# A two-layer decoder step: one more z unit ahead of the first convolution group, a shorter step-size series, two copies moved to ScalarE, and a new order where attention ends

## The chip, the core and the metric

The kernel runs on one core of a Trainium2 chip. The metric is the time of one execution on the device in microseconds (us). A matmul engine (TensorE, PE in the profile), VectorE (DVE), ScalarE (ACT), GpSimd (POOL) and the queue of SyncE (SP) run their own instruction streams, in order, and wait for each other on semaphores.

## The reference, cut to what matters

A Mamba-2 layer and an attention layer, each between two half-size SwiGLU blocks, work on 256 prompt tokens and 8 decode tokens side by side (N = 264 columns everywhere). The change touches the mixers of both.

```python
z, xbc, dt_raw = split(u @ w_in)                       # stage "sin": 49 units of weights
conv = conv_b + sum(xbc_full[:, k:k + t_len] * conv_w[k] for k in range(4))
xbc_act = silu(conv)
dt = softplus(dt_raw + dt_bias)                        # the step sizes, 32 heads
cum = cumsum(dt * a)                                   # per chunk of 128 tokens
decay = exp(where(causal, cum_t - cum_s, -inf))        # then the chunk products
...
s = einsum(q, k) * 64 ** -0.5                          # stage "q", with the shared K/V
prob = softmax(concat([s, sink]))[..., :-1]
out = einsum(prob, v) @ w_o                            # stage "o"
```

## The kernel before, in words

All weights are cut into 128x1024 units that stream through a ring of four buffers: SP loads `raw`, ScalarE rounds it to `whi` (L1080), VectorE subtracts to get `wlo` (L1552), and TensorE multiplies each unit in three passes (L503 to L505), 24 matmuls for a unit. The function `ahead(stage, i, j)` on ScalarE and on VectorE prepares the unit that lies four places on; ScalarE's waits until TensorE has finished unit j.

Stage "sin" is written out by hand in slots `s_`, one unit a slot; `SIN` lists what the slots hold: the step sizes (`dt`), then z units, then groups of four convolution units (c0 to c3, c4 to c7, ...) with z units between. In a slot TensorE runs `sin_unit`, VectorE reads the finished bank (`take`, L1599) and, for the convolution unit before it, runs three taps (`conv_taps`, L1827); ScalarE runs the last tap ahead of them (`tap_last`, L1254) and the silu behind them (`conv_silu`, L1260). From the seventh unit on two banks alternate, so unit j may start only when unit j-2 has been read:

```python
                if j < 7:
                    pe.wait_ge(b_free, sin_bank(j) + 1)
                else:
                    pe.wait_ge(a_free, A0["sin"] + (j - 2 if j < 9 else j + 3))
```

The step sizes go their own way beside that: VectorE computes the softplus by a series of dependent steps on 128x66 (`dt_start`, `dt_series`, `dt_end`, L1796 to L1811), ScalarE gathers them (`gather_sizes`, `gather_steps`), TensorE turns them (`pre_tokens`, slot `PRE_AT`), VectorE copies them out of the bank (L1841, L1842), TensorE forms the sums over tokens (`pre_sums`, from L952), ScalarE copies those (`cum4`, L1368), VectorE makes `tok` and the differences (`pre_sums`, L1853 to L1858; `pre_diff`, L1866), and the first chunk's exponentials follow on ScalarE (`decay_exp(0)`).

In attention eight pairs of heads run as a pipeline: `scores(t)` on TensorE (L667), `maxima(t)` on VectorE (L2090 on), `exps(t)` on ScalarE (L1469), which then puts the mask back into the banks (L1475), `probabilities(t)` on VectorE (L2102 to L2105), `transposes(t)` (L681), `copy_turned(t)` (L1480), `weighted_sum(t)`. The next pairs' rotary turn is `head_mean`, `rope_sin` (L1741) and `rope_add` (L1747) on VectorE. Behind the last queries come `embed_piece(n)` (six matmuls of another projection each) and the decode tokens' attention: `decode_scores` needs the queries that GpSimd spreads (`spread_queries`, L2399, which waits for the last `rope_add`); `decode_maxima` (from L2057), `decode_exp` and `decode_prob` follow. The order is that of the code on each engine.

Of the kernel before, what the change touches and what calls it, by code (L numbers as in the profile page):

```python
# [84 lines left out]
DT_STEPS = 15  # L85
# [5 lines left out]
Z_FIRST = [0, 1, 2]  # L91
Z_AFTER = {0: [3, 4], 1: [5], 2: [6], 3: [7], 4: [8], 5: [9], 6: [10], 7: [11, 12, 13, 14, 15]}
# [6 lines left out]
PRE_AT = 7  # L99
# [65 lines left out]
def trunk_kernel(nc, weights, xT, g1, pT, cst, vec, convst, ssm0, kcT, vc_in, ck, cv,  # L165
# [3 lines left out]
    with ExitStack() as ctx:  # L169
# [102 lines left out]
        pre_d = sem("pre_d")  # L272
        pre_a = sem("pre_a")
# [217 lines left out]
        def _(pe):  # L491
# [455 lines left out]
            def pre_sums():  # L947

                pe.wait_ge(pre_d, 1)
                for c in range(2):  # L950
                    dta = da4[c][:, 0:HEADS]
                    pe.matmul(bank[5][:, 64 * c:64 * c + 32], tri, dta, start=True, stop=True)  # L952
                    pe.matmul(bank[5][:, 64 * c + 32:64 * c + 64], ones, dta, start=True, stop=True)
                    mm = pe.matmul(bank[2][:, 128 * c:128 * c + 128], da4[c], tri, start=True, stop=True)
                mm.then_inc(pre_p, 1)
                pe.wait_ge(pre_d, 2)
                pe.matmul(bank[7][:, 0:256], ones[32:64, :], dgl[32:64], start=True, stop=True)
                pe.matmul(bank[6][:, 0:256], ones[0:32, :], dgl[0:32], start=True, stop=True).then_inc(pre_p, 1)
# [11 lines left out]
            for s_ in range(len(SIN)):  # L970
                if s_ == 1:
                    unit_pair("sin", 0)
                elif s_ > 1:
                    sin_unit(s_)
                if s_ == PRE_AT:
                    pre_tokens()
                if s_ == PRE_AT + 3:
                    pre_sums()
                for g in range(G):
                    if s_ == CHUNK_AT[g] + 3:  # L980
                        add_inter(g)
# [12 lines left out]
                if s_ - 1 in DEC_AT:  # L994
                    decode_columns(DEC_AT.index(s_ - 1))
# [52 lines left out]
            transposes(5)  # L1048
            decode_scores()
            weighted_sum(5)  # L1050
            embed_piece(2)
# [21 lines left out]
        def _(act):  # L1073
# [204 lines left out]
            def select(k):  # L1278

                g, c = k // 2, k % 2  # L1280
                if k == 1:
                    act.wait_ge(pre_d, 5)
# [45 lines left out]
            for s_ in range(SLOTS):  # L1328
# [11 lines left out]
                if 1 < s_ < len(SIN) and s_ != 5:  # L1340
                    ahead("sin", 0, s_)
                if s_ == 4:
                    ahead("sin", 0, 5)
                    gather_sizes()
                if kind == "conv":
# [3 lines left out]
                if s_ == 4:  # L1349
# [16 lines left out]
                if s_ == PRE_AT + 3:  # L1366
                    act.wait_ge(pre_p, 2)
                    act.activation(cum4, bank[2][:, 0:256], ACT.Copy).then_inc(pre_a, 1)  # L1368
                if s_ == PRE_AT + 5:
                    act.wait_ge(pre_d, 4)  # L1370
                    act.wait_ge(pre_const, 1)
                    select(0)
                    act.activation(tok[:, :, :, :], tok[:, :, :, :], ACT.Exp).then_inc(pre_a, 1)
# [172 lines left out]
        def _(dve):  # L1546
# [246 lines left out]
            def dt_series(ks):  # L1793

                for k in ks:
                    dt_step(dve.scalar_tensor_tensor(out=a_, in0=a_, scalar=1.0 / k, in1=s2_, op0=ALU.add, op1=ALU.mult))  # L1796

            def dt_start():
# [6 lines left out]
                dt_step(dve.tensor_scalar(a_, s2_, 1.0 / 17, None, ALU.mult))  # L1805
# [31 lines left out]
            def pre_tokens():  # L1837

                dve.wait_ge(pre_p, 1)
                for c in range(2):  # L1840
                    dve.tensor_copy(dtT[c], bank[4][:, 64 * c + 32:64 * c + 64])  # L1841
                    ins = dve.tensor_copy(da4[c].rearrange("p (k h) -> p k h", k=4), bank[4][:, 64 * c:64 * c + 32].unsqueeze(1).to_broadcast([P, 4, HEADS]))  # L1842
                ins.then_inc(pre_d, 1)
# [109 lines left out]
            for s_ in range(SLOTS):  # L1953
# [26 lines left out]
                if s_ == PRE_AT + 3:  # L1980
                    pre_sums()
                if s_ == PRE_AT + 4:
                    pre_diff(0)
                    pre_diff(1)
                if s_ == PRE_AT + 6:
# [567 lines left out]
```

## Time and profile before

| what | value |
|---|---|
| median of 3 executions | 1197.99 us (1197.15, 1197.99, 1199.66) |
| the profiled execution | 1199.46 us |
| its span, first to last instruction | 1197.6 us |
| PE busy | 1184.5 us (99%) |
| DVE, ACT, POOL busy | 866.2, 699.1, 245.1 us |
| 200 to 300 us (first part of "sin") | PE 98.45, DVE 93.22, ACT 75.93 us busy |
| 900 to 960 us (attention) | PE 57.06, DVE 47.56, ACT 46.63 us busy, mean granted clock 0.97 |

Busy time of PE holds short gaps between pipelined matmuls too, so what counts is when one unit starts after another: 2.90 us when nothing holds it. The profiled execution lies 1.47 us above the median.

### The profile page before, as it was taken

Reading aid. Unit: us, or ns where it says so; the run is one execution under the profiler, and the core shown is the slowest. Engines: PE = TensorE matmul, PEld = TensorE weight load, DVE = VectorE, ACT = ScalarE, POOL = GpSimd, SP = SyncE. Lnnn points to the kernel's source line nnn. Section 1 sums busy time; section 2 is a strip of 40 time slices with the busy share of each in tenths; the row PEclk is TensorE's granted clock in tenths of the full one; section 3 lists DMA queues with packets and bytes.
Section 4 is the critical chain, followed back from the end, with each engine's and each line's share of the span. In section 5 each row is a group of like instructions: output and inputs, shape, how many; then the busy total and the mean of one; then the engine's idle time right before and its main releaser. Section 6 shows DMA issues by size and latency. Waiting matters only on the chain.

```text
span 1197.6 us, 26532 instructions
## 1 busy us (share of the span) xinstructions
PE 1184.5 (99%) x9785; PEld 1156.7 (97%) x9785; DVE 866.2 (72%) x1382; ACT 699.1 (58%) x1148; POOL 245.1 (20%) x352
## 2 busy tenths in 40 slices
PE   9999999999999999999999999999999999999998
PEld 8999999998989899999999999999999899999998
DVE  7667646999899768766745987887468767667448
ACT  6454435787686657555546765555369664444345
POOL 1000002412222202122344333232036310000001
PEclk9999999999999999999999999999999999999999
DMA  8765554755445375867786677657742256555552
GB/s 298 240 209 184 176 178 140 259 184 186 159 149 189 108 225 185 329 211 251 283 294 225 215 276 282 211 184 240 251 141 94 90 171 212 176 179 189 176 178 87
DMA packets 63298, 239.90 MB, mean 200 GB/s; under 512 B 7673, under 2 KB 9633, under 8 KB 58849
## 3 DMA queue, kind: packets, MB, share of 16 engines
q1 hardware_dynamic: 56880, 197.83, 49.5%
q0 software_dynamic: 6064, 40.66, 9.4%
q8 instruction: 41, 0.67, 0.2%
q10 hardware_dynamic: 288, 0.54, 0.1%
q14 instruction: 25, 0.20, 0.0%
HBM read 226.87 MB, written 13.39 MB: 201 GB/s over the span
## 4 chain that ended last, share of the span: by engine, by line
PE 79%; DVE 8%; issue 5%; ACT 5%; DMA 1%; POOL 1%; SPq 0%; DVEq 0%; POOLq 0%; ACTq 0%
PE bank L503 24%; PE bank L504 24%; PE bank L505 24%; ACT whi L1080 2%; DVE wlo L1552 2%; DVE gu L1611 1%; DVE gu L1599 1%; DMA raw<-weights 1%; PE bank L873 1%; PE bank L868 1%; DVE xl L1571 1%; PE bank L895 1%; POOL sq L2179 0%; PE bank L681 0%; DVE xl L1700 0%
## 5 line engine op out<-in xcount | busy, mean ns | idle before, releaser
L1552 DVE TENSOR_TENSOR wlo<-raw,whi 128x1024 fp32r<-128x1024 f32 x367 | 456.3, 1247 | 241.5 <-ACT whi L1080 240.0
L503 PE MATMUL bank<-xh,whi 128*128 128x264 f32 x2008 | 576.1, 287 | 3.3 <-DVE under L1599 1.5
L504 PE MATMUL bank<-xl,whi 128*128 128x264 f32 x2008 | 569.2, 283 | 0.0
L505 PE MATMUL bank<-xh,wlo 128*128 128x264 f32 x2008 | 568.8, 283 | 0.0
L1080 ACT ACTIVATE whi<-raw 128x1024 fp32r<-128x1024 f32 x367 | 385.4, 1054 | 244.3 <-PE bank L505 235.5
L503 PEld LDWEIGHTS bank<-xh,whi 128*128 128x128 f32 x2008 | 378.2, 188 | 7.1 <-DVE wlo L1552 2.7
L504 PEld LDWEIGHTS bank<-xl,whi 128*128 128x128 f32 x2008 | 378.4, 188 | 0.9
L505 PEld LDWEIGHTS bank<-xh,wlo 128*128 128x128 f32 x2008 | 376.6, 188 | 0.0
L503 PE MATMUL bank<-hh,whi 128*128 (+1 forms) x896 | 255.5, 285 | 0.3 <-ACT gu L1435 0.3
L505 PE MATMUL bank<-hh,wlo 128*128 (+1 forms) x896 | 255.0, 285 | 0.0
L504 PE MATMUL bank<-hl,whi 128*128 (+1 forms) x896 | 254.4, 284 | 0.0
L503 PEld LDWEIGHTS bank<-hh,whi 128*128 128x128 f32 x896 | 168.6, 188 | 1.4 <-issue 0.8
L504 PEld LDWEIGHTS bank<-hl,whi 128*128 128x128 f32 x896 | 169.1, 189 | 0.1
L505 PEld LDWEIGHTS bank<-hh,wlo 128*128 128x128 f32 x896 | 168.6, 188 | 0.0
L1146 ACT ACTIVATE hh<-gu 128x264 fp32r<-128x264 f32 (+1 forms) x88 | 37.4, 425 | 168.5 <-DVE gu L1611 168.5
L2179 POOL TENSOR_TENSOR sq<-sq 128x264 f32<-128x264 f32 x49 | 39.7, 811 | 452.0 <-ACT sq L1118 446.7
L1599 DVE TENSOR_TENSOR gu<-bank,rstd 128x264 f32<-128x264 f32 x192 | 82.1, 429 | 16.0 <-PE bank L505 13.1
L1616 DVE TENSOR_TENSOR hl<-gu,hh 128x264 f32 (+1 forms) x88 | 39.6, 450 | 28.7 <-ACT hh L1146 28.7
L2328 POOL TENSOR_TENSOR xact<-xact,da_bc 128x512 f32<-128x512 f32 x32 | 37.8, 1183 | 101.6 <-PE bank L505 99.9
L1827 DVE SCALAR_TENSOR_TENSOR xact<-under,vs,xact 128x256 f32<-128x256 f32 x96 | 47.3, 493 | 2.3
L1611 DVE TENSOR_TENSOR gu<-gu 128x264 f32<-128x264 f32 x88 | 44.2, 502 | 0.0
L2333 POOL TENSOR_TENSOR xact<-xact 128x512 f32<-128x512 f32 x20 | 29.0, 1452 | 60.2 <-PE bank L505 56.4
(333 smaller groups left out, 1017.6 us busy)
## 6 DMA issues: line engine op xcount, KB each, us to landing
raw<-weights SPq DMA_DIRECT2D x367, 512.0 KB, 3.5
under<-ssm POOLq DMA_DIRECT2D x8, 1024.0 KB, 6.9
xact<-ssm POOLq DMA_DIRECT2D x8, 1024.0 KB, 7.2
out_ssm_s<-xact POOLq DMA_DIRECT2D x8, 1024.0 KB, 6.0
xact<-dtx_rows POOLq DMA_DIRECT2D x5, 1024.0 KB, 10.4
zs<-dtx_rows POOLq DMA_DIRECT2D x2, 1024.0 KB, 13.5
x<-xT SPq DMA_DIRECT2D x4, 264.0 KB, 5.5
xact<-stat_rows POOLq DMA_DIRECT2D x2, 528.0 KB, 6.5
```

What stands on the lines that cost most here:

```text
L503: pe.matmul(out, whi[:, w, c], rh, start=start, stop=False)
L504: pe.matmul(out, whi[:, w, c], rl, start=False, stop=False)
L505: return pe.matmul(out, wlo[:, w, c], rh, start=False, stop=stop)
L1080: act.activation(whi[:, s, :], raw[:, s, :], ACT.Copy).then_inc(hi_ready, 1)
L1146: act.activation(dst, gu[:, 2 * p + 1, :], ACT.Copy).then_inc(hh_ready, 1)
L1552: dve.tensor_tensor(wlo[:, s, :], raw[:, s, :], whi[:, s, :].bitcast(F32), ALU.subtract).then_inc(lo_ready, 1)
L1599: dve.tensor_tensor(dst, src[:, 0:N], rstd[:, :], ALU.mult).then_inc(a_free, 1)
L1611: dve.tensor_tensor(gu[:, 2 * p + 1, :], gu[:, 2 * p, :], gu[:, 2 * p + 1, :], ALU.mult).then_inc(h_ready, 1)
L1616: dve.tensor_tensor(one(hl), gu[:, 2 * p + 1, :], one(hh).bitcast(F32), ALU.subtract).then_inc(hl_ready, 1)
L1827: dve.scalar_tensor_tensor(out=out, in0=xr[:, k:k + T], scalar=vs[:, V_CW + CT * k + c:V_CW + CT * k + c + 1], in1=out, op0=ALU.mult, op1= ...
L2179: pool.tensor_tensor(sq3[:, 0, :], sq3[:, 0, :], sq3[:, m, :], ALU.add).then_inc(sq_pair, 1)
L2328: pool.tensor_tensor(by_head(part), by_head(part), da_bc[:, 2 * k:2 * k + 2, 4 * q:4 * q + 4].unsqueeze(3).to_broadcast([P, 2, 4, 64]), AL ...
```

## The change

In "sin" the first convolution group starts one slot later, behind four z units in place of three, and one z unit fewer stands behind it; from slot 9 on the slots hold the same units. The series has three steps on fitted coefficients in place of seven. `PRE_AT` goes from 7 to 8: VectorE's diagonal products, its sums and differences keep or change their slots as below and now stand ahead of the taps of their slot; the copies of the turned step sizes go from VectorE to ScalarE. In attention the order of some calls changes.

```diff
-DT_STEPS = 15
-Z_FIRST = [0, 1, 2]
-Z_AFTER = {0: [3, 4], 1: [5], ...
+DT_STEPS = 11
+ATANH = (0.14006083166778943, 0.14000885871391391, 0.20010764547514603, 0.33333208128558084)
+Z_FIRST = [0, 1, 2, 3]
+Z_AFTER = {0: [4], 1: [5], ...
-PRE_AT = 7
+PRE_AT = 8
@@ TensorE
-                pe.wait_ge(pre_d, 1)
+                pe.wait_ge(pre_t, 1)
...
-                if s_ == PRE_AT + 3:
+                if s_ == PRE_AT + 2:
                     pre_sums()
...
+            embed_piece(2)
             decode_scores()
             weighted_sum(5)
-            embed_piece(2)
@@ ScalarE, slots
-                if 1 < s_ < len(SIN) and s_ != 5:
+                if 1 < s_ < len(SIN) and s_ != 6:
                     ahead("sin", 0, s_)
-                if s_ == 4:
-                    ahead("sin", 0, 5)
+                if s_ == 5:
+                    ahead("sin", 0, 6)
                     gather_sizes()
+                if s_ == PRE_AT + 3:
+                    act.wait_ge(pre_p, 2)
+                    act.activation(cum4, bank[2][:, 0:256], ACT.Copy).then_inc(pre_a, 1)
+                if s_ == PRE_AT + 1:
+                    act.wait_ge(pre_p, 1)
+                    for c in range(2):
+                        act.activation(dtT[c], bank[4][:, 64 * c + 32:64 * c + 64], ACT.Copy)
+                        ins = act.activation(da4[c].rearrange("p (k h) -> p k h", k=4), bank[4][:, 64 * c:64 * c + 32]...)
+                    ins.then_inc(pre_t, 1)
+                if s_ == PRE_AT + 5:
+                    act.wait_ge(pre_d, 3)
+                    act.wait_ge(pre_const, 1)
+                    select(0)
+                    act.activation(tok[:, :, :, :], tok[:, :, :, :], ACT.Exp).then_inc(pre_a, 1)
                 if kind == "conv":
                     tap_last(s_, i)
@@ ScalarE, attention
             exps(6)
-            decode_exp()
             high_o(5)
             embed_copy(2)
+            decode_exp()
             copy_turned(6)
@@ VectorE, slots
+                if s_ == PRE_AT:
+                    pre_tokens()
+                if s_ == PRE_AT + 3:
+                    pre_sums()
+                if s_ == PRE_AT + 4:
+                    pre_diff(0)
+                    pre_diff(1)
                 if last == "conv":
                     conv_taps(li)
...
-                    dt_series((15, 13, 11, 9))
+                    dt_series(ATANH[1:])
                 if s_ == 3:
-                    dt_series((7, 5, 3))
                     dt_end()
-                if s_ == PRE_AT + 1:
-                    pre_tokens()
-                if s_ == PRE_AT + 3:
-                    pre_sums()
...
@@ VectorE, attention
             ahead("q", 0, 5)
+            probabilities(5)
             head_mean(7)
             rope_sin(7)
             rope_add(7)
-            probabilities(5)
-            low_o(4)
             maxima(6)
             decode_products()
+            low_o(4)
+            probabilities(6)
             decode_maxima()
-            probabilities(6)
             low_o(5)
```

ScalarE in stage "sin", from the silu of c2 on. Before, the silu of c2, `whi` for slot 8, then the silu of c3 and the next `whi`:

```order
L1260 ACTIVATE xact<-xact 128x256 [waits conv_sum]
L1080 ACTIVATE whi<-raw 128x1024 [waits unit_used,raw_landed2]
L1260 ACTIVATE xact<-xact 128x256 [waits conv_sum]
L1080 ACTIVATE whi<-raw 128x1024 [waits unit_used,raw_landed3]
L1265 ACTIVATE zs<-zs 128x264 [waits a_free]
L1270 ACTIVATE dact<-gu 128x32 [waits dec_sum]
L1275 ACTIVATE under<-gu 128x2x4 [waits dec_pad]
```

In the changed kernel, where the slots are one later, the same stretch (`small<-bank` are the moved copies):

```order
L1262 ACTIVATE xact<-xact 128x256 [waits conv_sum]
L1082 ACTIVATE whi<-raw 128x1024 [waits unit_used,raw_landed3]
L1353 ACTIVATE small<-bank 128x32 [waits pre_p]
L1354 ACTIVATE small<-bank 128x128
L1353 ACTIVATE small<-bank 128x32
L1354 ACTIVATE small<-bank 128x128
L1262 ACTIVATE xact<-xact 128x256 [waits conv_sum]
L1082 ACTIVATE whi<-raw 128x1024 [waits unit_used,raw_landed0]
```

The four copies now stand behind the silu of c2 and the `whi` of slot 9.

VectorE in stage "sin", from the read of c4 to about the read of c6 (`under<-bank` is the read of a convolution unit, `tok` and `hl<-bank` are the sums, `hl<-hl` the differences). Before:

```order
L1599 TENSOR_TENSOR under<-bank,rstd 128x264 [waits unit_used,tail_copied]
L1552 TENSOR_TENSOR wlo<-raw,whi 128x1024 [waits hi_ready]
L1853 COPY tok<-bank 128x2x32 [waits pre_p]
L1854 COPY tok<-bank 128x2x32
L1855 TENSOR_TENSOR tok<-tok 128x2x32 [waits dve_step]
L1858 TENSOR_TENSOR hl<-bank,hl 32x256 [waits pre_a]
L1858 TENSOR_TENSOR hl<-bank,hl 32x256
L1599 TENSOR_TENSOR under<-bank,rstd 128x264 [waits unit_used,tail_copied,dve_step]
L1827 SCALAR_TENSOR_TENSOR xact<-under,vs,xact 128x256 [waits conv_first]
L1827 SCALAR_TENSOR_TENSOR xact<-under,vs,xact 128x256 [waits conv_sum] x2
L1552 TENSOR_TENSOR wlo<-raw,whi 128x1024 [waits hi_ready]
```

In the changed kernel:

```order
L1608 TENSOR_TENSOR under<-bank,rstd 128x264 [waits unit_used,tail_copied]
L1858 COPY tok<-bank 128x2x32 [waits pre_p]
L1859 COPY tok<-bank 128x2x32
L1860 TENSOR_TENSOR tok<-tok 128x2x32 [waits dve_step]
L1863 TENSOR_TENSOR hl<-bank,hl 32x256 [waits pre_a]
L1863 TENSOR_TENSOR hl<-bank,hl 32x256
L1836 SCALAR_TENSOR_TENSOR xact<-under,vs,xact 128x256 [waits conv_first,dve_step]
L1836 SCALAR_TENSOR_TENSOR xact<-under,vs,xact 128x256 [waits conv_sum] x2
L1561 TENSOR_TENSOR wlo<-raw,whi 128x1024 [waits hi_ready]
L1608 TENSOR_TENSOR under<-bank,rstd 128x264 [waits unit_used,tail_copied]
```

The sums stood ahead of the read of c5, and now stand behind it, ahead of the taps.

VectorE at attention's end, from the `wlo` of `ahead("q", 0, 5)` on. Before (L1730 and L1731 are `head_mean(7)`, L2102 on is `probabilities(5)`, L2090 on is `maxima(6)`):

```order
L1552 TENSOR_TENSOR wlo<-raw,whi 128x1024 [waits hi_ready]
L1730 TENSOR_SCALAR small<-bank 128x1 [waits r_ready,rot_done]
L1731 TENSOR_TENSOR small<-bank,zs 128x4
L1741 TENSOR_TENSOR gu<-under 128x264 [waits q_swapped1]
L1747 TENSOR_TENSOR xact<-gu 128x264 [waits q_sin,q_cos]
L2102 TENSOR_TENSOR small<-small 128x4 [waits s_exp]
L2103 RECIPROCAL small<-small 128x4 [waits dve_step]
L2104 TENSOR_TENSOR under<-under,small 128x2x128 [waits dve_step]
L2105 TENSOR_TENSOR under<-under,small 128x2x256
L2110 TENSOR_TENSOR hl<-bank,hh 128x256 [waits hh_ready]
L2090 TENSOR_REDUCE small<-bank 128x2 [waits s_done]
```

In the changed kernel (L2106 on is `probabilities(5)`, L1739 and L1740 `head_mean(7)`, L2094 `maxima(6)`):

```order
L1561 TENSOR_TENSOR wlo<-raw,whi 128x1024 [waits hi_ready]
L2106 TENSOR_TENSOR small<-small 128x4 [waits s_exp]
L2107 RECIPROCAL small<-small 128x4 [waits dve_step]
L2108 TENSOR_TENSOR under<-under,small 128x2x128 [waits dve_step]
L2109 TENSOR_TENSOR under<-under,small 128x2x256
L1739 TENSOR_SCALAR small<-bank 128x1 [waits r_ready,rot_done]
L1740 TENSOR_TENSOR small<-bank,zs 128x4
L1750 TENSOR_TENSOR gu<-under 128x264 [waits q_swapped1]
L1756 TENSOR_TENSOR xact<-gu 128x264 [waits q_sin,q_cos]
L2094 TENSOR_REDUCE small<-bank 128x2 [waits s_done]
```

The four instructions of `probabilities(5)` went ahead of the rotary turn of the last pair, and `low_o(4)` left the place ahead of `maxima(6)`.

## Rows read from the trace of the kernel before

**Rows 1.** The page, part 1: busy us (share of the span) and instructions.

```profile
PE 1184.5 (99%) x9785; PEld 1156.7 (97%) x9785; DVE 866.2 (72%) x1382; ACT 699.1 (58%) x1148; POOL 245.1 (20%) x352
```

**Rows 2.** Waits of PE: us in total, times, longest.

```profile
PE bank L503 <- DVE under L1599: 1.5, 1, 1.5
PE bank L681 <- DVE under L2105: 1.4, 1, 1.4
PE bank L667 <- ACT bank L1475: 1.3, 3, 0.7
```

**Rows 3.** Timeline of PE in "sin": start, us, instruction, [idle before].

```profile
230.61 0.36 PE L503 MATMUL bank<-xh,whi 128*128 128x264 f32 x1 [1.50 <-DVE under L1599]
...
241.83 0.28 PE L503 MATMUL bank<-xh,whi 128*128 128x264 f32 x1
...
251.56 0.28 PE L503 MATMUL bank<-xh,whi 128*128 128x264 f32 x1
```

**Rows 4.** Timeline of DVE in "sin".

```profile
218.51 1.10 DVE L1796 SCALAR_TENSOR_TENSOR xact<-xact 128x66 f32<-128x66 f32 x4
...
227.12 0.43 DVE L1599 TENSOR_TENSOR under<-bank,rstd 128x264 f32<-128x264 f32 x1
227.47 1.52 DVE L1827 SCALAR_TENSOR_TENSOR xact<-under,vs,xact 128x256 f32<-128x256 f32 x3
228.90 1.22 DVE L1552 TENSOR_TENSOR wlo<-raw,whi 128x1024 fp32r<-128x1024 f32 x1
230.03 0.43 DVE L1599 TENSOR_TENSOR under<-bank,rstd 128x264 f32<-128x264 f32 x1
...
236.51 0.83 DVE L1845 TENSOR_TENSOR xact<-cs,small 32x256 f32<-32x256 f32 x2
...
240.33 0.22 DVE L1853 COPY tok<-bank 128x64 f32<-128x64 f32 x1
...
240.97 0.86 DVE L1858 TENSOR_TENSOR hl<-bank,hl 32x256 fp32r<-32x256 f32 x2
242.13 0.43 DVE L1599 TENSOR_TENSOR under<-bank,rstd 128x264 f32<-128x264 f32 x1 [0.30 <-PE bank L505]
...
249.87 0.42 DVE L1599 TENSOR_TENSOR under<-bank,rstd 128x264 f32<-128x264 f32 x1
```

**Rows 5.** Timeline of ACT in "sin".

```profile
234.90 0.42 ACT L1260 ACTIVATE xact<-xact 128x256 f32<-128x256 f32 x1 [1.60 <-DVE xact L1827]
235.22 1.05 ACT L1080 ACTIVATE whi<-raw 128x1024 fp32r<-128x1024 f32 x1
...
240.14 0.36 ACT L1368 ACTIVATE hl<-bank 128x256 fp32r<-128x256 f32 x1
```

**Rows 6.** Timeline of PE in attention.

```profile
933.64 0.70 PE L667 MATMUL bank<-xact 64*128 64x256 f32 x4 [0.72 <-ACT bank L1475]
...
935.96 1.17 PE L681 MATMUL bank<-cs,under 128*128 128x128 f32 x6 [1.39 <-DVE under L2105]
```

**Rows 7.** Timeline of PE behind `decode_turn`.

```profile
947.17 0.36 PE L503 MATMUL bank<-ph,whi 128*128 128x264 f32 x1
```

**Rows 8.** Timeline of DVE and ACT in attention.

```profile
934.47 0.16 DVE L2102 TENSOR_TENSOR small<-small 128x4 f32<-128x4 f32 x1
...
936.15 0.41 DVE L2090 TENSOR_REDUCE small<-bank 128x2 f32<-128x256 f32 x1
...
937.86 0.45 ACT L1469 ACTIVATE under<-bank,small 128x128 f32<-128x128 f32 x1
...
940.06 0.81 ACT L1475 ACTIVATE bank<-cs 128x768 f32<-128x768 f32 x1
```

**Rows 9.** Timeline of POOL, `spread_queries`, first call (x2).

```profile
923.46 0.78 POOL L2399 TENSOR_SCALAR under<-xact,cs 128x32 f32<-128x32 f32 x2
```

**Rows 10.** The same, second call.

```profile
934.65 1.43 POOL L2399 TENSOR_SCALAR under<-xact,cs 128x32 f32<-128x32 f32 x2 [1.37 <-DVE xact L1747]
```

**Rows 11.** Windows: stretch, us, busy of PE, PEld, DVE, ACT, POOL, granted clock, DMA.

```profile
936.40:939.80 3.40, 3.40 (x30) 3.07 (x30) 1.63 (x7) 2.64 (x9) 3.07 (x8) 0.50 0.03 12
```

More of the change, by code:

```diff
@@ L82 @@
 NV = V_QS + 1
-DT_STEPS = 15
-Z_FIRST = [0, 1, 2]
-Z_AFTER = {0: [3, 4], 1: [5], 2: [6], 3: [7], 4: [8], 5: [9], 6: [10], 7: [11, 12, 13, 14, 15]}
+DT_STEPS = 11
+ATANH = (0.14006083166778943, 0.14000885871391391, 0.20010764547514603, 0.33333208128558084)
+Z_FIRST = [0, 1, 2, 3]
+Z_AFTER = {0: [4], 1: [5], 2: [6], 3: [7], 4: [8], 5: [9], 6: [10], 7: [11, 12, 13, 14, 15]}
 SIN = [("dt", 0)] + [("z", _t) for _t in Z_FIRST]
@@ L272, in trunk_kernel @@
         pre_d = sem("pre_d")
+        pre_t = sem("pre_t")
         pre_a = sem("pre_a")
@@ L955, in pre_sums @@
                 mm.then_inc(pre_p, 1)
-                pe.wait_ge(pre_d, 2)
+                pe.wait_ge(pre_d, 1)
                 pe.matmul(bank[7][:, 0:256], ones[32:64, :], dgl[32:64], start=True, stop=True)
@@ L1281, in select @@
                 if k == 1:
-                    act.wait_ge(pre_d, 5)
+                    act.wait_ge(pre_d, 4)
                 if k >= 2:
@@ L1339, in _ @@
                         decay_exp(2 * CHUNK_AT.index(s_))
-                if 1 < s_ < len(SIN) and s_ != 5:
+                if 1 < s_ < len(SIN) and s_ != 6:
                     ahead("sin", 0, s_)
-                if s_ == 4:
-                    ahead("sin", 0, 5)
+                if s_ == 5:
+                    ahead("sin", 0, 6)
                     gather_sizes()
+                if s_ == PRE_AT + 3:
[5 more added lines that the diff above has]
+                        act.activation(dtT[c], bank[4][:, 64 * c + 32:64 * c + 64], ACT.Copy)
+                        ins = act.activation(da4[c].rearrange("p (k h) -> p k h", k=4), bank[4][:, 64 * c:64 * c + 32].unsqueeze(1).to_broadcast([P, 4, HEADS]), ACT.Copy)
+                    ins.then_inc(pre_t, 1)
[4 more added lines that the diff above has]
+                    act.activation(tok[:, :, :, :], tok[:, :, :, :], ACT.Exp).then_inc(pre_a, 1)
                 if kind == "conv":
@@ L1348, in _ @@
                     decay_exp(2 * CHUNK_AT.index(s_))
-                if s_ == 4:
+                if s_ == 5:
                     gather_steps()
@@ L1365, in _ @@
                     copy_rows(DEC_AT.index(s_))
-                if s_ == PRE_AT + 3:
-                    act.wait_ge(pre_p, 2)
-                    act.activation(cum4, bank[2][:, 0:256], ACT.Copy).then_inc(pre_a, 1)
                 if s_ == PRE_AT + 5:
[L1370 to L1373, printed above, removed]
                     act.wait_ge(pre_p, 3)
@@ L1795, in dt_series @@
                 for k in ks:
-                    dt_step(dve.scalar_tensor_tensor(out=a_, in0=a_, scalar=1.0 / k, in1=s2_, op0=ALU.add, op1=ALU.mult))
+                    dt_step(dve.scalar_tensor_tensor(out=a_, in0=a_, scalar=k, in1=s2_, op0=ALU.add, op1=ALU.mult))
             def dt_start():
@@ L1804, in dt_start @@
                 dt_step(dve.tensor_tensor(s2_, q_, q_, ALU.mult))
-                dt_step(dve.tensor_scalar(a_, s2_, 1.0 / 17, None, ALU.mult))
+                dt_step(dve.tensor_scalar(a_, s2_, ATANH[0], None, ALU.mult))
             def dt_end():
@@ L1837, in pre_tokens @@
             def pre_tokens():
[L1839 to L1843, printed above, removed]
+                dve.wait_ge(dt_a_step, 5)
                 for k in (0, 32):
@@ L1973, in _ @@
                 if s_ == 2:
-                    dt_series((15, 13, 11, 9))
+                    dt_series(ATANH[1:])
                 if s_ == 3:
-                    dt_series((7, 5, 3))
                     dt_end()
-                if s_ == PRE_AT + 1:
-                    pre_tokens()
-                if s_ == PRE_AT + 3:
-                    pre_sums()
[L1982 to L1985, printed above, removed]
+                if s_ == PRE_AT + 5:
                     pre_decode()
```

## The prediction, as it was made before the changed kernel ran

> **What bounds the kernel now.** I read part 1 of the page first. PE is busy for 1184.5 us of a span of 1197.6 [rows 1], so whatever is done elsewhere, the time can only fall by what PE now loses; no matmul is added or taken away. The view of waits then says where PE loses: apart from the start, one wait of 1.5 us for a read by VectorE (L1599), one of 1.4 us for L2105 and three that add up to 1.3 us for L1475 [rows 2]. The timeline places the first in "sin" at 228.8 to 230.6 us [rows 3], the others in attention around 933 to 936 us [rows 6]. A third view, the windows, shows a loss that no wait names: from 936.4 to 939.8 us, just behind two idle stretches of 0.72 and 1.39 us, the granted clock is 0.50 [rows 11], so the score matmuls of the decode tokens run at 1.2 GHz and not at 2.4.
>
> **Stage "sin", why PE waits there.** From c0 on, a VectorE slot is a read, three taps and one `wlo`: 227.12 to 230.03, which is 2.91 us [rows 4]. A unit on PE takes 2.90 us. VectorE therefore never catches up in these slots, and the series of the step sizes had put it behind. Unit 9 needs the read of unit 7, which is c3's at 230.03 to 230.46; PE had been ready at 228.95, and starts at 230.61 [rows 3, 4]. It loses 1.66 us.
>
> **What the first part of the change gives.** Four dependent steps fall away. Four took 1.10 us [rows 4], so everything behind comes 1.1 us sooner. And c3 is now unit 8, not unit 7, so that unit 9 needs only c2's read. In order: the read of z3 at about 221.7 (c0's was at 222.7), then read and `wlo` without taps, 0.35 + 1.13 = 1.48 us, gives c0's read at 223.15 and c1's at 224.6; c1's slot with taps and 0.6 us of waiting for the first tap, which on ScalarE stands behind `whi` and the gather, gives c2's read at 228.2, done at 228.6. PE wants unit 9 at 228.95. **Minus 1.66 us**, and with 0.3 us to spare.
>
> **The copies on ScalarE.** They stand behind the silu of c2 and the `whi` of slot 9, as the order shows. On VectorE c3's read is at 231.1, the diagonal products now come ahead of the taps (0.83 us [rows 4]) and the taps of c2 end at 231.5 + 0.86 + 1.52 = 233.85. ScalarE's silu starts behind them and `whi` 0.32 us later (234.90 to 235.22 [rows 5]); `whi` holds it 0.97 more. The four copies begin at 235.15. Their price is not in the trace: the read of a bank of 256 columns takes 0.36 us (at 240.14, [rows 5]); these have 32 and 128 columns. From below, 4 x 0.1 = 0.4 us, since instructions overlap; from above 4 x 0.36 = 1.4. I take 0.65. So TensorE gets `pre_t` at about 235.8. It gets through units 9 and 10 at 228.95 + 5.8 + 0.1 = 234.9. **Plus 1.0 us** (0.8 to 1.8). What is queued behind that wait is unit 11 and all that follows on PE.
>
> **The sums behind c5's read.** Before, VectorE did them at 240.33 to 241.83 and then still waited 0.30 us for PE to finish c5; they were hidden [rows 4]. Now they stand behind that read, and so do `cum4`'s copy and, on ScalarE, a `whi` that waits for the same unit ahead of it. From c5's read to c7's it took 242.13 to 249.87, 7.74 us. Added: 1.42 us of sums, and 0.37 us in which the last two of them wait for `cum4` (`whi` starts 0.26 us after unit 12, lasts 0.97, the copy 0.36, which ends 1.6 us after unit 12; VectorE is there at 0.30 + 0.35 + 0.64 = 1.3). So c7's read ends 0.30 + 7.74 + 1.79 + 0.42 = 10.25 us after unit 12 starts, and PE starts unit 15, which needs it, 0.14 us on, at 10.39. Now unit 15 starts 251.56 - 241.83 = 9.73 us after unit 12 [rows 3]. **Plus 0.65 us** (0.3 if ScalarE were not late with `cum4`).
>
> The later steps of that chain have room: the first chunk's exponentials follow c7's last tap and come about 0.75 us later than now against the clock of the trace, where the product that waits for them had over 1 us. "Sin" thus adds up to -1.66 + 1.0 + 0.65, or about **0**, and I count -0.1 for a small wait of the same read kind before the sixteenth unit that goes.
>
> **Attention.** `probabilities(5)` started at 934.47, behind the turn of the last pair, which had waited for its swapped rows; now it starts right behind `wlo`, at 932.9, and ends at 934.3. That is when PE is through with `scores(6)` (933.64 + 0.72). The wait of 1.39 us [rows 6] goes. What is late next: `rope_add(7)` ends at 935.3 and not 934.55, and GpSimd's spreading waits for it. Its two instructions took 0.78 us at 923.46 and 1.43 us at 934.65 [rows 9, 10]; in the first case VectorE ran the same reductions as it will here, so I take 0.78 and both ends for the range. `decode_scores` starts at 936.3 (937.0). PE has the transposes and, newly, `embed_piece(2)` (0.93 us) until 936.0, and waits 0.3 to 1.0 us. Then the chain leaves PE: `maxima(6)` starts at 935.25 and not 936.15, `exps(6)` at 936.7 and not 937.86, and ends 2.18 us later; the mask (0.81 us [rows 8]) lets `scores(7)` start at 939.9; `probabilities(6)` (1.35 us), `decode_maxima` (1.11 us) and `low_o(5)` (0.34 us) bring VectorE from 938.95 to `maxima(7)` at 941.7, whose 1.4 us let `exps(7)` begin at 943.1. It ends at 945.3, and the sixth `embed_piece`, which needs it, starts at 945.4. It started at 947.17 [rows 7]. **Minus 1.8 us**, against the profiled execution.
>
> Part of that is the clock. At half rate for 3.41 us, PE lost at most 1.7 us. Laid out at full rate, the old order reaches the same `embed_piece` at 945.85, since maxima and exponentials then set the pace: the clock cost 1.3 us and the change brings 0.45 without it. In the new order the idle stretches at 932.9 (0.72 us) and 936 (0.3 to 1.0 us) lie four microseconds apart from end to end and hold less than the 2.1 us that came before the fall; the 1.5 us of idle time at 229 us were followed by none. So I expect full clock, 2.4 GHz, throughout. The Trainium skill (TensorE: Matmul & The Clock Gate, Terms) puts the price at the throttled time times (1 - K/N), here 3.41 x 0.5 = 1.7 us; by it the sum would be 0.4 us lower where the fall goes. The rows give 1.3, because waits hide the rest, and I use that.
>
> **The sum.** Against the profiled execution: 1199.46 - 0.1 - 1.8 = 1197.6. Its time is 1.47 us above the median of the runs, near the highest (1199.66), about the clock's 1.3 us. If the executions at 1197.15 and 1197.99 had no fall, the sum from the median is 1197.99 - 0.1 - 0.45 = 1197.4. The two agree; I say **1197.4**. 0.2% of the time, 2.4 us, is about what can be told from no change.
>
> **Rivals.** *The new waits in "sin" stay away* (chance 0.2): the copies cost 0.4 us and ScalarE runs earlier than I lay out, or VectorE gains on its slots. Then up to 1.65 us more come off: 1195.8, and 1194.5 if all executions of before had the fall. Against it speaks that `whi` and silu stand ahead of the copies in any case. *The clock falls in the new order as well* (0.2): the stretches between 932.9 and 943 still hold idle time of some 2 us in all. Then the 0.45 and 1.3 us are taken back in part: 1198.2. *Slower* (0.08): the wait for `pre_t` at 235 us, of 1 to 1.8 us, is joined by that for c7's read and by the first chunk's product, behind c7's tap on ScalarE, and the clock falls behind one of them; 3.4 us of dense matmuls at half rate cost 1.7. With 0.6 to 0.9 of additional waiting that is 1197.4 + 2.5 = 1199.9; it decides from a `pre_t` later than 236.6. It did not fall behind 1.5 us of waiting at 229. *The forecast* has 0.52.
>
> **Range.** The forecast's own is 1196.6 to 1198.4 (copies 0.4 to 1.4, spreading 0.78 or 1.43, the fall in some executions). To leave out two in ten, it goes down into the first rival, to 1195.6, and up into the others, to 1199.2. Faster by over 0.2%, below 1195.6: 0.16, most of it the first rival. Slower, above 1200.4: 0.05. Within: 0.79.
>
> **What would show it.** In the new trace: no wait for L1608 (the read) at 229 us; a wait of TensorE for the copies (L1354) of about 1 us near 235, where the sums start; one of 0.3 to 0.7 us for a read near 250; in attention none for L2109 at 934, short ones ahead of `decode_scores` and `scores(7)`, `embed_piece(5)` 1.8 us earlier against `scores(6)`, and a granted clock of 1.00 throughout. I am wrong if the copies run ahead of 235 us, if the sums' place costs nothing, or if the half clock is there again.

## The result and the profile after

| | before | after |
|---|---|---|
| median | 1198.15 us (1197.15 to 1200.17, 19 executions) | 1199.81 us (1198.82 to 1201.48, 19 executions) |
| ratio after / before | | 1.0013, 95% interval 1.0007 to 1.0019 |
| the profiled execution, its span | 1199.46, 1197.6 us | 1200.99, 1199.2 us |

The changed kernel is 1.7 us slower, where the prediction said 1197.4 us and gave 1195.6 to 1199.2 as its range. By the bound of 0.2% that is no change; by the interval it is a small loss.

The page of the changed kernel, part 1, answers to [rows 1]: the same matmuls, eight fewer instructions on VectorE, four more on ScalarE.

```profile
PE 1185.2 (99%) x9785; PEld 1157.1 (96%) x9785; DVE 865.9 (72%) x1374; ACT 700.1 (58%) x1152; POOL 244.8 (20%) x352
```

The waits of PE in the changed kernel from 225 to 262 us. The wait for the read at 229 us [rows 2] is gone, and three others are there, 2.98 us together.

```profile
PE bank L854 <- ACT hl L1287: 1.2, 1, 1.2
PE bank L954 <- ACT small L1354: 1.0, 1, 1.0
PE bank L846 <- DVE sq L1907: 0.8, 1, 0.8
```

The timeline of PE in the changed kernel, against [rows 3]. Unit 9 starts at once. The unit behind the first chunk's work starts at 260.04 us; before, at 256.67.

```profile
228.97 0.36 PE L505 MATMUL bank<-xh,whi 128*128 128x264 f32 x1
...
236.00 0.41 PE L954 MATMUL bank<-small,cs 128*128 128x32 f32 x2 [0.97 <-ACT small L1354]
...
253.46 0.50 PE L854 MATMUL bank<-hl 128*128 128x512 f32 x1 [1.24 <-ACT hl L1287]
...
257.87 0.38 PE L846 MATMUL bank<-xact 128*128 128x128 f32 x1 [0.77 <-DVE sq L1907]
...
260.04 0.36 PE L505 MATMUL bank<-xh,whi 128*128 128x264 f32 x1
```

VectorE in the changed kernel, against [rows 4]. It idles for 3.34 us in front of c5's read, and only then come the sums. Before, the sums stood at 240.33 us, inside such idle time.

```profile
243.01 0.43 DVE L1608 TENSOR_TENSOR under<-bank,rstd 128x264 f32<-128x264 f32 x1 [3.34 <-PE bank L507]
243.36 0.21 DVE L1858 COPY tok<-bank 128x64 f32<-128x64 f32 x1
...
244.36 0.86 DVE L1863 TENSOR_TENSOR hl<-bank,hl 32x256 fp32r<-32x256 f32 x2 [0.40 <-ACT hl L1349]
...
247.95 0.43 DVE L1608 TENSOR_TENSOR under<-bank,rstd 128x264 f32<-128x264 f32 x1
...
249.24 0.68 DVE L1871 TENSOR_TENSOR hl<-hl,cs 64x512 fp32r<-64x512 f32 x1
...
250.20 1.52 DVE L1836 SCALAR_TENSOR_TENSOR xact<-under,vs,xact 128x256 f32<-128x256 f32 x3
```

ScalarE in the changed kernel, against [rows 5]. The copies end at 235.95. Later, the silu of c5 waits 2.73 us for VectorE's taps, and `whi` (1.04), the selected differences (L1287), the table load (1.28) and the exponentials stand behind it in that order.

```profile
235.66 0.29 ACT L1354 ACTIVATE small<-bank 128x128 f32<-128x128 f32 x1
...
251.75 0.42 ACT L1262 ACTIVATE xact<-xact 128x256 f32<-128x256 f32 x1 [2.73 <-DVE xact L1836]
252.08 1.04 ACT L1082 ACTIVATE whi<-raw 128x1024 fp32r<-128x1024 f32 x1
253.03 0.39 ACT L1287 ACTIVATE hl<-hl,cs 128x128 fp32r<-128x128 f32 x1
253.43 1.28 ACT L1360 ACT_TABLE_LOAD   x1
254.72 0.36 ACT L1360 ACTIVATE tok<-tok 128x192 f32<-128x192 f32 x1
```

Windows of the changed kernel, columns as in [rows 11]. Behind the wait at 235 us and the short matmuls of the sums the granted clock is 0.50 (1.2 GHz) for 3.4 us. In attention, where [rows 11] had it, it is 1.00 (2.4 GHz).

```profile
234.40:237.70 3.30, 2.33 (x20) 1.99 (x20) 3.23 (x6) 2.20 (x8) 0.00 (x0) 1.00 0.94 300
237.75:241.15 3.40, 3.40 (x16) 2.75 (x15) 1.92 (x3) 1.80 (x5) 1.16 (x1) 0.50 0.80 277
937.05:941.90 4.85, 4.64 (x54) 4.16 (x54) 3.64 (x14) 3.36 (x11) 2.79 (x8) 1.00 0.36 108
```

PE and POOL in attention in the changed kernel. The wait of 1.39 us for L2105 [rows 6] is gone, and GpSimd's spreading takes 0.77 us and not 1.43 [rows 10]. The embedding unit that started at 947.17 [rows 7] starts at 948.72, 11.70 us behind `scores(6)` and not 13.53.

```profile
937.02 0.70 PE L669 MATMUL bank<-xact 64*128 64x256 f32 x4 [0.72 <-ACT bank L1484]
...
939.69 1.97 PE L712 MATMUL bank<-xact,under 128*64 128x128 f32 x32 [0.21 <-POOL under L2403]
...
943.21 0.70 PE L669 MATMUL bank<-xact 64*128 64x256 f32 x4 [0.43 <-ACT bank L1484]
...
948.72 0.36 PE L505 MATMUL bank<-ph,whi 128*128 128x264 f32 x1 [0.40 <-ACT small L1481]
938.78 0.77 POOL L2403 TENSOR_SCALAR under<-xact,cs 128x32 f32<-128x32 f32 x2 [2.12 <-DVE xact L1756]
```

**Clock falls.** One execution has a stretch at 1.2 GHz and the next of the same kernel has none; below, "a fall" is such a stretch amid the work. The mean clock of the span shows it in part. The seven traces with a mean of 0.998 (before, after, kernels 2, 5, 6, 7 and 8 below) have one fall each; the five at 1.000 (4 and 9 to 12) and the two at 0.999 (1 and 3) have none. Ten of the fourteen also end at half clock behind the last matmul, both at 0.999 among them, so 0.999 can come from that alone; whether it can also hide a fall no trace shows. Of 99 executions of the kernel before, 24 are at 0.998, with a median of 1199.4 us, and the other 75 have 1197.9. Of 19 after, 4 are at 0.998 (median 1201.2); the other 15 have 1199.67. The table below gives both.

### The profile page after: what moved, and what is told of

Same layout as the page of the kernel before. It is cut to its first block, busy times and chain, and to the rows that moved or that the text cites. A ratio compares the mean times of both kernels' runs of the same rounds, so it can differ in the third digit from the quotient of the medians.

```text
span 1199.2 us, 26529 instructions
## 1 busy us (share of the span) xinstructions
PE 1185.2 (99%) x9785; PEld 1157.1 (96%) x9785; DVE 865.9 (72%) x1374; ACT 700.1 (58%) x1152; POOL 244.8 (20%) x352
## 4 chain that ended last, share of the span: by engine, by line
PE 91%; DVE 4%; ACT 3%; issue 1%; POOL 1%; DMA 0%; SPq 0%; ACTq 0%; DVEq 0%; POOLq 0%
PE bank L505 28%; PE bank L506 28%; PE bank L507 28%; ACT whi L1082 1%; DVE wlo L1561 1%; PE bank L875 1%; DVE xact L1836 1%; PE bank L870 1%; PE bank L897 1%; ACT under L1478 1%; DMA x<-xT 0%; POOL sq L2183 0%; PE bank L927 0%; DVE xl L1580 0%; PE bank L669 0%
```

## The experiments

Each kernel ran 11 times, beside 33 executions of the kernel before (medians 1197.99, 1198.13 and 1198.21 us for kernels 1 to 4, 5 to 8 and 9 to 12). "Stretch" is taken in the profiled execution, from when PE is ready for unit 9 (its wait ahead of it included) to the start of the unit behind the first chunk's work. PE does the same work in it in every kernel. Its two ends by themselves do not compare, since PE is ready for unit 9 anywhere between 228.50 and 229.69 us.

| kernel | median | ratio, 95% interval | at 0.998 or less | median of the rest | waits of PE, 225 to 262 us | stretch |
|---|---|---|---|---|---|---|
| before | | | 24 of 99 | 1197.9 | 1.5 | 27.72 |
| after | 1199.81 | 1.0013 (1.0007 to 1.0019) | 4 of 19 | 1199.67 | 0.97, 1.24, 0.77 | 31.07 (a fall) |
| 1 attention only | 1197.87 | 0.9997 (0.9988 to 1.0006) | 1 | 1197.8 | as before | 27.72 |
| 2 "sin" only | 1200.32 | 1.0019 (1.0010 to 1.0028) | 7 | 1199.4 | as after | 29.50 |
| 3 z order, series | 1196.89 | 0.9987 (0.9978 to 0.9996) | 0 | 1196.9 | 0.5 | 26.48 |
| 4 = 3 + attention | 1196.67 | 0.9988 (0.9979 to 0.9997) | 0 | 1196.7 | 0.5 | 26.47 |
| 5 after, copies on VectorE | 1198.20 | 1.0001 (0.9992 to 1.0010) | 2 | 1198.1 | 1.25, 0.78 | 28.29 |
| 6 after, selection early | 1199.66 | 1.0012 (1.0003 to 1.0022) | 3 | 1199.5 | 1.0, 0.7, 1.1 | 30.76 (a fall) |
| 7 after, exponentials early | 1200.70 | 1.0019 (1.0010 to 1.0028) | 7 | 1199.4 | 1.0, 0.3, 0.9 | 29.04 |
| 8 = 3 + copies in slot 8 | 1196.88 | 0.9986 (0.9977 to 0.9995) | 5 | 1196.2 | none | 25.96 |
| 9 = 8 + attention | 1195.85 | 0.9982 (0.9973 to 0.9991) | 2 | 1195.8 | none | 25.95 |
| 10 after, copies in slot 8 | 1198.58 | 1.0002 (0.9993 to 1.0011) | 0 | 1198.6 | 1.24, 0.78 | 28.29 |
| 11 after, sums back | 1199.25 | 1.0001 (0.9992 to 1.0010) | 2 | 1198.6 | 0.95, 0.34 | 27.51 |
| 12 = 10 + 11 | 1197.32 | 0.9992 (0.9983 to 1.0001) | 0 | 1197.3 | 0.60, 0.35 | 27.16 |

**1 and 2: the two places apart.** One is the kernel before with attention's new order, the other the changed kernel with attention's old order.

```diff
+            embed_piece(2)
             decode_scores()
             weighted_sum(5)
-            embed_piece(2)
...
```

> The kernel before, with the new order of attention alone on TensorE, ScalarE and VectorE. My theory (attention gains, stage sin loses): 0.45 us less than before in executions whose clock does not fall, up to 1.8 where it fell before, so a median of about 0.5 to 1 us less; the wait for probabilities(5) at 934 us is gone. Rival (the new order of attention is itself part of the loss, since two small waits take the place of one): no difference or up to 1 us more.

> The changed kernel with attention's order put back. My theory: stage sin alone costs 2.1 us without a fall of the clock (1.0 for the copies, 1.24 for select(0), 0.77 for the first chunk's product, less 1.66 for the old wait, and some for later places), so 1.8 to 2.5 us more than before, and more where the clock falls at 238 us. Rival (the loss is spread, or lies in attention): under 1 us more.

Attention alone changes nothing that can be measured (0.9997), less than the 0.45 us expected. "Sin" alone is slower by the whole amount, 1.0019, as expected. The loss is made in "sin". Kernel 2 has the "sin" of the changed kernel, and its profiled execution has no fall there (it has one at 950 us): its stretch is 29.50 us against 27.72 before, 1.8 more.

**3 and 4: the front of "sin" alone.** The kernel before with the three-step series and `c0` behind four z units; `PRE_AT`, copies, sums and differences stay as before. The fourth kernel has attention's order too.

```diff
-DT_STEPS = 15
-Z_FIRST = [0, 1, 2]
-Z_AFTER = {0: [3, 4],
+DT_STEPS = 11
+Z_FIRST = [0, 1, 2, 3]
+Z_AFTER = {0: [4],
```

> The kernel before, with the fourth z unit ahead of the first group and the three-step series, and nothing else: copies on VectorE, sums and differences in their old places. My theory (the old wait of 1.66 us goes by these two alone, and the loss is the moved chain): 1.4 to 1.7 us less than before, no wait of TensorE between 225 and 260 us above 0.2 us. Rival (one convolution group later leaves too little time for the first chunk whatever the chain does): new waits near 250 us eat it, 0 to 1 us less or more than before.

> The same with the new order of attention on top. My theory: both gains add, 2 to 2.5 us less than before (about 1196). Rival (a sooner end of stage sin is given back later, or attention's order gains nothing): no more than 1.5 us less.

This half gains about 1.1 us by its median (1.2 in the stretch), where 1.4 to 1.7 were expected. The wait of 1.5 us goes and one of 0.48 us, for a read again, comes ahead of the unit at 247.0 us. Kernel 4 is 1.3 us below the kernel before, not 2 to 2.5, which is what its rival said. So whatever loses is in the rest: the moved copies, sums, differences and exponentials.

**5: the copies.** The changed kernel with its four copies back on VectorE, in slot 8 ahead of the products.

```diff
@@ VectorE, pre_tokens
+                dve.wait_ge(pre_p, 1)
+                for c in range(2):
+                    dve.tensor_copy(dtT[c], ...)
+                    ins = dve.tensor_copy(da4[c]..., ...)
+                ins.then_inc(pre_t, 1)
```

> The changed kernel with the four copies back on VectorE, ahead of its diagonal products in slot 8. Theory A (the copies wait in ScalarE's queue behind a silu and a whi, and everything behind unit 11 moves with PE): the wait of 1.0 us at 235 us goes and nothing takes its place, since VectorE idles 3.3 us afterwards; 1.0 us less than the changed kernel without falls of the clock, about 1198.7. The waits for select(0) and for the first chunk's product stay at 1.2 and 0.8 us. Rival (TensorE only moves its waiting to the later chain): under 0.3 us less, the wait for select(0) grows to 2.2 us.

It measured 1198.2, 1.6 us less by the medians where 1.0 was expected, and 1.2 less in the stretch (28.29 against 29.50 in kernel 2): the wait of 0.97 us goes, and the profiled execution has no fall near it (it has one at 950 us). The other two waits stay, so they have another cause. This does not yet tell the engine from the slot, since VectorE made its copies a slot sooner.

**6 and 7: what stands ahead on ScalarE.** In 6, `select(0)` is put right behind slot 12's last tap, ahead of the silu of c5 and of `whi`; in 7, the selection and exponentials are one block at the end of slot 12, behind that silu and ahead of `whi`.

```diff
@@ ScalarE, kernel 6
                     tap_last(s_, i)
+                if s_ == PRE_AT + 4:
+                    act.wait_ge(pre_d, 3)
+                    act.wait_ge(pre_const, 1)
+                    select(0)
```

> The changed kernel with select(0) alone one slot sooner, between the last tap and the silu of slot 12. Theory A (the two waits at 252 and 257 us are one lateness: ScalarE's run of select, table load and exponentials behind the silu of c5 and the whi of slot 13): the wait of 1.24 us goes, the one ahead of chunk_in(1) grows from 0.8 to about 1.8 us, and only 0.3 to 0.5 us come off, about 1199.3. Rival (select(0) itself holds TensorE): 1.2 us less, about 1198.5.

> The changed kernel with the whole block of the first chunk (select(0), the exponentials, decay_exp(0)) at the end of slot 12, ahead of the whi and of the last tap of slot 13, where it stands in the kernel before. Theory A: the block starts 0.95 us sooner, the wait for select(0) falls to 0.3 us, the next stays near 0.7; 0.9 us less than the changed kernel, about 1198.8. Rival (the differences on VectorE, which come behind the sums, set the time of that block): under 0.3 us less.

Both gained less than expected. In 6 the selection ran at 249.67 and its wait went, but another grew and one for a read came. The view of PE's waits in kernel 6, 225 to 262 us:

```profile
PE bank L846 <- DVE sq L1908: 1.1, 1, 1.1
PE bank L954 <- ACT small L1354: 1.0, 1, 1.0
PE bank L505 <- DVE under L1609: 0.7, 1, 0.7
```

Of 2.0 us 1.75 are left: PE, no longer stopped at the selected differences, now stops at a read that VectorE makes late, and at the exponentials. The same view of kernel 7:

```profile
PE bank L954 <- ACT small L1354: 1.0, 1, 1.0
PE bank L505 <- DVE zs L1607: 0.9, 1, 0.9
PE bank L854 <- ACT hl L1287: 0.3, 1, 0.3
```

The wait for the selected differences fell to 0.3 us as laid out, and that for the products of the first chunk (L846) is gone; one of 0.9 us for VectorE's read of a z unit took its place. Its stretch is 29.04 us, 0.5 under kernel 2's. The rest of its executions has 1199.4; the median of 1200.7 comes from the seven with a fall. So the order on ScalarE mostly passes the delay on: it enters earlier, on VectorE.

**8: the copies on ScalarE, without the other moves.** Kernel 3 with the copies taken off VectorE, in slot 8 ahead of the last tap; the changed kernel has them in slot 9, behind `whi`.

```diff
@@ ScalarE
+                if s_ == PRE_AT + 1:        # 8, PRE_AT is 7 here
+                    act.wait_ge(pre_p, 1)
+                    for c in range(2):
+                        act.activation(dtT[c], ...)
+                        ins = act.activation(da4[c]..., ...)
+                    ins.then_inc(pre_t, 1)
```

> The kernel of the third run (fourth z unit and short series, rest as before) with the four copies on ScalarE, in slot 8 ahead of the last tap. Theory A (what costs is the place in the queue, behind slot 9's whi, not the engine): no wait of TensorE near 235 us, VectorE is relieved of 0.6 us, and the wait of 0.5 us at 246 us shrinks or goes: 1196.4 to 1196.9, no slower than the third run. Rival (ScalarE is too late with the copies wherever they stand): a wait near 235 us of 0.5 us or more, 1197.4 or above.

No wait of PE is left between 225 and 262 us, and executions without a sure fall have 1196.2, 0.7 less than kernel 3 (0.5 in the stretch). Moving the copies to ScalarE is itself a gain. Five executions have a fall, and the profiled one has it at 935.0 us, behind idle stretches of 0.69 and 1.48 us, as in the kernel before; so the median stands still.

**9: with attention's order.** Kernel 8 with the edit of 1.

> The kernel before with the step-size polynomial, the new z order, the four copies on ScalarE in slot 8 and attention's new order; sums and differences stay where they were before the change. Theory A (what the whole change loses comes from the slots to which copies, sums and differences were moved): 1196.1 us, 2.0 under the kernel before; the order of attention takes 0.1 to 0.2 from the executions without a clock fall and keeps the fall at 935 us away, so at most 1 of 11 executions at a mean clock of 0.998. Rival: the order of attention only moves the fall; then as many executions with one as in the run with z order, polynomial and copies (5 of 11) and 1196.9.

1195.85 us, the best of all: 2.4 us below the kernel before by the medians (2.2 by the ratio, 0.9982). Two of eleven executions still have a fall, one more than expected; the rival's five are not there, though eleven executions against eleven do not settle that.

**10: one slot for the copies.** The changed kernel, with one figure changed.

```diff
@@ ScalarE
-                if s_ == PRE_AT + 1:
+                if s_ == PRE_AT:
                     act.wait_ge(pre_p, 1)
```

> The whole change, with the four copies on ScalarE one slot earlier, ahead of slot 8's last tap instead of behind the weights of slot 9. Theory A: they then end some 5 us ahead of the sums, TensorE's wait of 0.98 us at 236.0 is gone, and with it the clock fall at 237.7: 1198.4 us (1.0 to 1.5 under the whole change); the waits of 1.24 us for the selected differences and 0.77 us for the decay products stay. Rival B: ScalarE as such is too full here, the copies hold up its last tap of slot 8 and the silu behind it, and a wait of about 1 us comes at a later unit: 1199.5.

As theory A had it: 1.2 us under the changed kernel by the medians and 1.2 under kernel 2 in the stretch. None of eleven executions is at 0.998; beside four of 19 that does not show that the wait brings the fall, and the 1.2 us need no fall. The timeline of ScalarE in kernel 10: the copies end at 232.8, 2.7 us ahead of the sums (PE is there at 235.49) and not 5, and the silu behind them still waits for VectorE.

```profile
232.19 0.17 ACT L1353 ACTIVATE small<-bank 128x32 f32<-128x32 f32 x1
...
232.49 0.29 ACT L1354 ACTIVATE small<-bank 128x128 f32<-128x128 f32 x1
232.65 0.62 ACT L1256 ACTIVATE xact<-under,vs 128x256 f32<-128x256 f32 x1
234.70 0.42 ACT L1262 ACTIVATE xact<-xact 128x256 f32<-128x256 f32 x1 [1.43 <-DVE xact L1836]
```

**11: the sums and differences back.** The changed kernel with both behind the taps of the slot before, and with the copy of the turned sums at that slot's end.

```diff
@@ VectorE
-                if s_ == PRE_AT + 3:
-                    pre_sums()
-                if s_ == PRE_AT + 4:
-                    pre_diff(0)
-                    pre_diff(1)
                 if last == "conv":
                     conv_taps(li)
...
+                if s_ == PRE_AT + 2:
+                    pre_sums()
+                if s_ == PRE_AT + 3:
+                    pre_diff(0)
+                    pre_diff(1)
```

> The whole change, with VectorE's sums and differences put back behind the taps of the slot before (slots 10 and 11 instead of ahead of the taps of 11 and 12), and ScalarE's copy of the turned sums with them. Theory A: ahead of the taps of a slot is behind that slot's read, and the read waits for TensorE; back in the slot before, they fill VectorE's idle 3.34 us, the differences end about 4 us earlier, and both waits (1.24 and 0.77 us) are gone: 1197.7 us. The wait of 0.98 us for the copies stays. Rival B: the sums come from TensorE late because of that wait, VectorE stands at them, and the read of unit 10 or 11 behind them makes TensorE wait instead: over 1199.

The timeline of VectorE in kernel 11. Sums and differences run ahead of the reads, and the differences end at 245.9 and not at 250.2.

```profile
239.22 0.22 DVE L1858 COPY tok<-bank 128x64 f32<-128x64 f32 x1
...
239.86 0.86 DVE L1863 TENSOR_TENSOR hl<-bank,hl 32x256 fp32r<-32x256 f32 x2
241.11 0.43 DVE L1608 TENSOR_TENSOR under<-bank,rstd 128x264 f32<-128x264 f32 x1 [0.39 <-PE bank L507]
...
244.97 0.68 DVE L1871 TENSOR_TENSOR hl<-hl,cs 64x512 fp32r<-64x512 f32 x1
```

The wait for the selected differences is gone, that for the decay products fell from 0.77 to 0.34 us, that for the copies stays at 0.95; the stretch is 27.51 us, 2.0 under kernel 2's. The four executions at a clock of 1.000 have 1196.9 to 1198.1 us, as theory A had it; the other seven lie at 1198.6 to 1199.7, and so does the median, which missed. They are as far above as a fall costs elsewhere, but their mean clocks (0.999 for five, 0.998 for two) show it only for two.

**12: both.** The edits of 10 and 11 in one kernel.

> Both of the last two edits in the whole change. Theory A: the three waits are each their own, so the gains add: 1196.3 us (1195.9 to 1196.8), level with the kernel of z order, polynomial, copies and attention. Rival: the two share a cause (the late sums), so that the sum of the gains is less than 2.5 us: 1197.2 or more.

1197.32: the rival's case. The two gains do not add up in full; in the stretch they are 1.2 and 2.0 us alone and 2.3 together. PE's waits in kernel 12, 225 to 262 us:

```profile
PE bank L505 <- DVE under L1608: 0.6, 1, 0.6
PE bank L846 <- DVE sq L1907: 0.4, 1, 0.4
```

With PE no longer held at 235 us, a read that stands behind the differences is late, as in kernels 3 and 4; and the exponentials, which keep their new place behind a `whi`, still hold the decay products; that it is their place was not tested from here. Neither wait is in kernel 9, 1.5 us lower, which keeps the old place of the exponentials and of the diagonal products too. Of that 1.5 us, 1.2 lie in the stretch; the rest was not taken apart.

## Why the prediction was wrong

- *Minus 1.66 us for unit 9*: right. It starts at 228.97 us with no wait.
- *The copies on ScalarE, plus 1.0 us*: right, 0.97 (1.2 with the restart, by kernels 2 and 10). Predicted to begin at 235.15 and to cost 0.65 us, they ran from 235.35 to 235.95, 0.60 us. Kernel 10 shows that the slot makes that wait and not the engine.
- *The sums behind c5's read, plus 0.65 us, through c7's read*: the delay was right and its outlet wrong. c7's read started 9.76 us behind c5's and not 7.74 [rows 4], 2.0 more where 1.79 was laid out. But the wait of 0.3 to 0.7 us for a read near 250 us never came, since PE was stopped elsewhere.
- *"The later steps of that chain have room"*: this is the step that failed. It put the first chunk's exponentials 0.75 us later. Counted from c5's read, the selection, which starts their block, came at 10.02 us and not at 7.05, 3.0 us later, by the rows below and those of the changed kernel above. The sums take 1.90 us behind that read (243.36 to 245.26, 0.40 of it waiting for `cum4`), and so c5's taps and silu come 2.0 us later; `whi`, now ahead of the selection, adds 0.95. Before, the selected differences were ready 1.4 us before PE used them (249.57, 251.00). Now PE waits 1.24 us for them, and 0.77 us more for the products behind table load and exponentials. The differences stood ahead of c5's taps before too, so by these rows it is the sums' move that delays them; kernel 11 undoes both moves together, and the first wait and half of the second go. Kernels 6 and 7, which change only ScalarE's order, get 0.2 to 0.5 us back. So VectorE's moved work is shown to be the larger part; that the exponentials' place is the rest is only argued.

```profile
246.00 0.68 DVE L1866 TENSOR_TENSOR hl<-hl,cs 64x512 fp32r<-64x512 f32 x1
...
247.30 1.52 DVE L1827 SCALAR_TENSOR_TENSOR xact<-under,vs,xact 128x256 f32<-128x256 f32 x3
249.18 0.39 ACT L1285 ACTIVATE hl<-hl,cs 128x128 fp32r<-128x128 f32 x1
251.00 0.48 PE L852 MATMUL bank<-hl 128*128 128x512 f32 x1
```

- *Net of "sin", -0.1*: without a fall it is 29.50 - 27.72 = +1.8 us (kernel 2 against before), and the medians of executions without a sure fall differ by 1199.67 - 1197.9 = 1.7. The named waits give only -1.66 + 0.97 + 1.24 + 0.77 = +1.3: PE loses more at a wait than its idle time. Three waits of 2.98 us make the stretch 3.55 us longer than in kernel 9, which has none.
- *Attention, minus 1.8 us against the profiled execution*: 13.53 - 11.70 = 1.83 us, but by wrong terms, so the number was luck. From `transposes(5)` to the embedding unit the kernel before took 947.17 - 935.96 = 11.21 us with the fall [rows 6, 7]. Kernels 2 and 3 have the old order and no fall there, and took 9.66 (rows below). So the fall had cost 1.55 us and not 1.3. *0.45 us without the clock* is mis-sized: from `scores(6)` on, the old order without a fall takes 11.39 us in kernel 2 and 11.83 in kernel 3, the new order 11.69 to 11.74 in all ten traces that have it. The old order varies with the swapped rows that the last pair's turn on VectorE waits for (no idle time in kernel 2, 0.32 us in 3, 0.49 before); the new order gains 0.1 us on the one and loses 0.3 on the other. The pairs of kernels agree, by the median of the rest: 0.1 (before, 1), 0.2 (3, 4), 0.4 (8, 9), -0.3 (2, after). The spreading took 0.77 us as taken, and PE's wait ahead of it was 0.21 and not 0.3 to 1.0. The rows are of kernel 2, then of kernel 3:

```profile
935.02 0.70 PE L669 MATMUL bank<-xact 64*128 64x256 f32 x4 [0.72 <-ACT bank L1484]
936.75 0.88 PE L683 MATMUL bank<-cs,under 128*128 128x128 f32 x6 [0.80 <-DVE under L2109]
946.41 0.36 PE L505 MATMUL bank<-ph,whi 128*128 128x264 f32 x1
...
933.18 0.70 PE L668 MATMUL bank<-xact 64*128 64x256 f32 x4 [0.68 <-ACT bank L1476]
935.35 0.87 PE L682 MATMUL bank<-cs,under 128*128 128x128 f32 x6 [1.24 <-DVE under L2105]
945.01 0.36 PE L504 MATMUL bank<-ph,whi 128*128 128x264 f32 x1
```

- *Full clock throughout*: wrong in the profiled execution, where the fall moved to 237.7 us, behind the new wait of 0.97 us and the small matmuls of the sums; six of 19 executions have a mean of 1.000. The rival *slower*, to which I gave 0.08, had such a fall. That its price of 1199.9 is nearly the measured median is luck: the price counts 1.7 us for the fall, and the executions without a sure fall have 1199.67. Of its three waits two came, for `pre_t` and for the first chunk's product; c7's read did not hold PE, and the largest wait, for the selected differences, is in no rival.
- *The sum from the median*: it took 1197.99 as free of falls, which the 75 executions at 1197.9 bear out.

The price of the fall can be read in "sin" too. The stretch took 260.04 - 228.97 = 31.07 us in the changed kernel, with the fall. In kernel 2, with the same "sin" and no fall there, it took 258.00 - 228.50 = 29.50, so 1.57 us are the fall's. The Trainium skill (TensorE: Matmul & The Clock Gate, Terms) gives throttled time times (1 - K/N), here about 3.4 x 0.5 = 1.7 us, an estimate; the traces have 1.57 here and 1.55 in attention, close to it and slightly less. The prediction's 1.3, "because waits hide the rest", took off too much.

```profile
228.50 0.36 PE L505 MATMUL bank<-xh,whi 128*128 128x264 f32 x1
...
258.00 0.36 PE L505 MATMUL bank<-xh,whi 128*128 128x264 f32 x1
```

## What to carry to other kernels

"Ahead of the taps of a slot" is also "behind that slot's read", and a read waits for the engine that is the bound: before moving side work to another place in the code, look at which wait it lands behind, and whether it used to fill that wait's idle time. Follow a delay along every in-order queue that its results reach, with what stands ahead there, and look for the first place where the bounding engine needs one of them, not only for the place where it waited before. Here the same change with side work left in its old slots, and only the copies taken off the busy engine early, turns 1.7 us of loss into 2.4 us of gain.

## What the runs showed of the hardware that was not expected

The clock falls in some executions of one and the same program, in the profiled ones at one of a few places: at 936.4 us in the kernel before, 237.7 in the changed one, about 238.2 in kernel 6 (behind the same wait), 935.0 in 8, and near 950 us in 2, 5 and 7. Kernel 3 has nearly the idle stretches of the kernel before in attention (0.68 and 1.24 us) and no fall there. In kernel 7 the fall at 951.3 us had PE busy throughout the 3.35 us ahead of it, as its windows show; its last idle stretches were 0.49 and 0.41 us, ending at 944.5 and 947.1 us. So the idle stretches just ahead, by which I had placed the fall, do not tell where it comes, and I have no rule for it.

```profile
947.90:951.25 3.35, 3.35 (x75) 3.06 (x74) 2.22 (x5) 1.20 (x2) 0.00 (x0) 1.00 0.15 22
951.30:954.65 3.35, 3.35 (x21) 2.78 (x20) 2.46 (x6) 0.92 (x3) 0.00 (x0) 0.50 0.38 144
```

A fall costs 1.5 us of the whole time by the medians (24 executions against 75 of before; 4 against 15 after), and 1.3 to 1.8 us by the smaller groups of kernels 2 and 5 to 9. That is as much as the effects studied here, so the share of executions with a fall moves a median by itself: kernel 8, with five of eleven, has the median of kernel 3 though its other executions are 0.7 us lower.
